# Layer 1's closing stage with tokens on partitions instead of model columns

## The reference

```python
out = moe_ffn(hl2, router_w[i], router_b[i], exp_w_gate[i], exp_w_up[i], exp_w_down[i],
              sh_w_gate[i], sh_w_up[i], sh_w_down[i])      # routed experts + shared expert
xl = xl + g2 * out.reshape(b, n_lat, d)                     # g2: one gate value per column
...
return rms_norm(xl, final_norm_w)

def routed_experts(...):      # per block of rows of one expert
    out = swiglu(h_pad[tok], e_gate[e], e_up[e], e_down[e])
    return y.at[tok].add(out * wt[:, None]), None

def rms_norm(x, w):
    y = xf * lax.rsqrt(jnp.mean(xf * xf, axis=-1, keepdims=True) + NORM_EPS)
    return y.astype(x.dtype) * w
```

## Time and profile before

| | us |
|---|---|
| Median of 3 runs (lowest, highest) | 2405.94 (2404.68, 2408.18) |
| The profiled execution | 2402.2 |
| Its span, first to last instruction | 2400.4 |
| PE busy | 2174.2 (91%) |
| DVE busy | 910.6 (38%) |
| ACT busy | 566.3 (24%) |
| POOL busy | 674.1 (28%) |

### The profile page before, as it was taken

How to read it: one execution, slowest core, us unless ns; L and a number is a source line. 1 busy time by engine, 2 the same in 40 slices (tenths; PEclk the granted TensorE clock), 3 DMA queues, 4 the chain that set the end, 5 groups by cost and what they waited for, 6 DMA issues and landing times.

```text
span 2400.4 us, 36613 instructions
## 1 busy us (share of the span) xinstructions
PE 2174.2 (91%) x12802; PEld 1173.2 (49%) x12802; DVE 910.6 (38%) x1858; ACT 566.3 (24%) x1170; POOL 674.1 (28%) x811
## 2 busy tenths in 40 slices
PE   4998989898899999999997798899879998888997
PEld 1464344454555555555546463354355454444545
DVE  2186676315512222222226485663352211111117
ACT  4222154304211111111113522342211111111113
POOL 0000000000245555555540000000045555555530
PEclk8999999998899999999999899999989999999999
DMA  7522000018699999999969121000159999999977
GB/s 317 221 78 75 0 1 1 1 35 333 240 376 418 420 412 408 408 409 418 412 266 326 53 91 37 1 1 18 70 236 397 417 416 414 409 408 409 413 295 245
DMA packets 104857, 594.23 MB, mean 248 GB/s; under 512 B 25142, under 2 KB 29374, under 8 KB 62528
## 3 DMA queue, kind: packets, MB, share of 16 engines
q1 hardware_dynamic: 68656, 524.73, 54.1%
q0 software_dynamic: 34672, 63.07, 7.0%
q10 hardware_dynamic: 1440, 5.24, 0.6%
HBM read 572.94 MB, written 60.56 MB: 264 GB/s over the span
## 4 chain that ended last, share of the span: by engine, by line
PE 68%; DMA 18%; DVE 7%; ACT 3%; issue 2%; SPq 1%; POOL 0%; POOLq 0%; DVEq 0%; ACTq 0%
PE psum L1056 22%; PE psum L704 18%; DMA arena<-in_experts 13%; PE psum L1078 10%; PE psum L875 3%; PE psum L899 2%; DMA arena<-y 2%; PE psum L915 2%; DMA arena<-in_mod_w 2%; PE psum L787 2%; PE psum L813 2%; PE psum L1064 1%; DVE arena L1544 1%; PE psum L720 1%; PE psum L1122 1%
## 5 line engine op out<-in xcount | busy, mean ns | idle before, releaser
L1056 PE MATMUL psum<-arena 128*64 128x256 f32 x6144 | 715.5, 386 | 39.2 <-DMA arena<-in_experts 31.2
L1056 PEld LDWEIGHTS psum<-arena 128*64 128x64 f32 x6144 | 440.4, 138 | 252.6 <-issue 43.6
L704 PE MATMUL psum<-arena 128*128 128x512 f32 (+1 forms) x1360 | 503.7, 528 | 24.9 <-ACT arena L1180 12.7
L2085 POOL DMA_INDIRECT arena<-hrows,IX x384 | 394.1, 1026 | 228.1 <-POOL IX L2081 163.1
L704 PEld LDWEIGHTS psum<-arena 128*128 128x128 f32 x1360 | 259.6, 193 | 264.1 <-issue 235.0
L1078 PE MATMUL psum<-arena 128*64 128x512 f32 x1536 | 363.5, 593 | 6.9 <-DMA arena<-in_experts 5.7
L2093 POOL DMA_INDIRECT y<-arena,IX x192 | 197.1, 1027 | 305.7 <-DVE arena L1929 146.2
L1936 DVE TENSOR_TENSOR arena<-psum,arena 128x128 f32<-128x128 f32 x192 | 55.9, 291 | 503.9 <-ACT arena L1420 503.9
L1420 ACT ACTIVATE arena<-psum 128x128 f32<-128x128 f32 x192 | 53.3, 278 | 667.6 <-PE psum L1056 667.6
L1428 ACT ACTIVATE arena<-psum 128x512 f32<-128x512 f32 x192 | 114.7, 597 | 310.7 <-PE psum L1078 310.7
L1078 PEld LDWEIGHTS psum<-arena 128*64 128x64 f32 x1536 | 112.8, 137 | 144.1 <-issue 119.8
(11 more groups left out here) (245 smaller groups left out, 1740.2 us busy)
## 6 DMA issues: line engine op xcount, KB each, us to landing
arena<-in_experts SPq DMA_DIRECT2D x128, 2048.0 KB, 20.9
arena<-in_experts SPq DMA_DIRECT2D x128, 1024.0 KB, 23.7
arena<-in_mod_w SPq DMA_DIRECT2D x48, 1024.0 KB, 11.1
arena<-y SPq DMA_DIRECT2D x20, 1536.0 KB, 15.6
arena<-in_wblk SPq DMA_DIRECT2D x22, 1024.0 KB, 4.9
arena<-in_shared SPq DMA_DIRECT2D x2, 3072.0 KB, 10.4
arena<-hrows,IX POOLq DMA_INDIRECT x384, 8.0
hrows<-arena ACTq DMA_DIRECT2D x10, 512.0 KB, 8.7
```

What stands on the lines that cost most here:

```text
L704: last = mm(job(l, key, n, parts), a, b, start=i == 0, stop=i == len(pairs) - 1)
L1056: last = mm(psum[j * ROWS:(j + 1) * ROWS, (0, 1, 5)[u], 0:2 * P], HT[:, u, k, :], w[:, k * 512 + j * 256:k * 512 + (j + 1) * 256], start=k ...
L2085: g.indirect_dma_start(GR[:, r, h * 256:(h + 1) * 256], None, rows, offsets(IX[:, s, h:h + 1]), bounds_check=4 * T * P - 1, oob_is_err=Fal ...
```

## The change

It concerns layer 1 alone, apart from the arrays handed over.

- A new job `gate` stands first in layer 1's shared list. PE spreads the gate's 1024 values over rows by 8 matmuls, with tokens' rows on partitions (64 rows for columns 0 to 511, 64 for 512 to 1023), and ACT copies them to `G2`. The banks of the jobs behind it are one further on.
- In layer 1's expert loop `weighted` is DVE's: it multiplies the down product by `G2` as it writes `YB`. ACT has only `gates` left. On DVE it stands between `hidden` and `hidden_in`.
- The final norm's weights come as 128 equal rows (`final`, 512 KB) and are loaded to `FW` ahead of y.
- A transfer of y carries three of the six rows of its block whole (runs of 1024 f32), not all six by half.
- PE transposes X for all four blocks into the eight PSUM banks (`xt`, bank 2t + i, 32 matmuls), and adds the sums to it there by 3 matmuls of 512 columns each half, tokens on partitions. `gated` is gone.
- The norm goes by token rows: ACT squares both banks at once and sums along the row, then a root of one column; DVE takes its reciprocal and makes two products of 512 columns from PSUM with `FW`. The block goes out in rows of 1024 f32.

```diff
@@ class Plan
+        self.shared += ["gate"] if l else []
         tiles(6)
...
-            j += [(("ct", t, i), "D") for i in range(2)]
-            if l == LAYERS - 1:
-                j += [(("nf", t), "A")]
+            j += [(("ct" if l == 0 else "xt", t, i), "D") for i in range(2)]
...
+            elif k[0] == "xt":
+                bk = 2 * k[1] + k[2]
@@ sync
+                if l == LAYERS - 1:
+                    sp.dma_start(FW, A["final"]).then_inc(sem("final_in"), 16)
+                for t in range(pl.t_out if l == LAYERS - 1 else 0):
+                    if t >= 3:
+                        ready(sp, l, ("xt", t - 3, 1))
+                    rows = y6d[l].rearrange("(k t p c) d -> t p k (c d)", k=TOPK, p=P, c=2)[t]
+                    for i in range(2):
+                        sp.dma_start(Y6[:, t % 3, 3 * i:3 * i + 3, :], rows[:, 3 * i:3 * i + 3, :]).then_inc(sem(f"y6in{t % 3}{i}"), 16)
...
-                sp.wait_ge(sem(f"norm_used{l}"), pl.norm[("nf", t)] + 1)
-                sp.dma_start(out[:, :, t * P:(t + 1) * P], H[:, :, t * P:(t + 1) * P]).then_inc(sem("out_done"), 16)
+                evacuated(sp, l, ("xt", t, 1))
+                sp.dma_start(out[t * P:(t + 1) * P, :], O[t]).then_inc(sem("out_done"), 16)
@@ tensor
+                    elif st == "gate":
+                        start_job(st)
+                        for m in range(KC):
+                            q = m // 4
+                            last = mm(psum[q * ROWS:(q + 1) * ROWS, pl.bank[st], (m % 4) * P:(m % 4 + 1) * P],
+                                      modTs[l][:, 5 * KC + m, 0:1].to_broadcast([P, ROWS]), ident, start=True, stop=True)
+                        last.then_inc(done, 1)
...
+                if l == LAYERS - 1:
+                    evacuated(pe, l, ("sd", KC - 1, 0))
+                    for t in range(pl.t_out):
+                        for i in range(2):
+                            start_job(("xt", t, i))
+                            for k in range(4):
+                                mm(job(l, ("xt", t, i))[:, k * P:(k + 1) * P], X[:, 4 * i + k, t * P:(t + 1) * P], ident,
+                                   start=k == 0, stop=False)
+                    for t in range(pl.t_out):
+                        for i in range(2):
+                            pe.wait_ge(sem(f"ysum{l}"), 2 * t + i + 1)
+                            for y in range(3):
+                                last = mm(job(l, ("xt", t, i)), ident, Y6[:, t % 3, y, i * 512:(i + 1) * 512], start=False, stop=y == 2)
+                            last.then_inc(done, 1)
@@ scalar
+                    elif st == "gate":
+                        ready(act, l, st)
+                        f(G2[:, :], job(l, st), ACT.Copy).then_inc(evacA, 1)
...
-                        for i in range(2):
-                            evacuated(act, l, ("ct", t, i))
-                            n = pl.square[("nf", t)][0] + i
-                            act.wait_ge(sem(f"sq_used{l}"), n - 2)
-                            f(SQB[:, n % 3, :].rearrange("p (k c) -> p k c", k=4), X[:, 4 * i:4 * i + 4, t * P:(t + 1) * P],
-                              ACT.Square).then_inc(sem(f"sq_ready{l}"), 1)
-                        root(("nf", t), P)
+                        ready(act, l, ("xt", t, 1))
+                        f(JUNK, psum[:, 2 * t:2 * t + 2, :].rearrange("p b n -> p (b n)"), ACT.Square, accum_out=ssq[:, t:t + 1]
+                          ).then_inc(sem("sum_made"), 1)
+                        act.wait_ge(sem("sum_made"), t + 1)
+                        f(rms[:, t:t + 1], ssq[:, t:t + 1], ACT.Sqrt, bias=epsb[:, 0:1], scale=1.0 / D).then_inc(sem("rms"), 1)
@@ vector
+                def weighted(s, i):
+                    dve.wait_ge(sem(f"down{l}"), i * n + (s + 1))
+                    r, u = tour.place(s, tour.y_ring)
+                    dve.wait_ge(sem(f"scat{r}_{l}"), i * 16 * tour.uses(r, tour.y_ring) + (16 * u + scat0))
+                    dve.sem_inc(sem("passed"), 1)
+                    V.tensor_tensor(YB[:, r, :], psum[:, (3, 4, 6)[tour.third(s)], :], G2[:, :], ALU.mult).then_inc(sem(f"y_a{l}"), 1)
...
                             hidden(ahead, i * n + (s + 1))
+                        if l:
+                            weighted(s, i)
+                        if not (last_round and ahead == 0):
                             hidden_in(ahead, i * n + (s + 1))
...
                 def last_norm(t):
-                    r = recip(("nf", t), P)
-                    for k in range(KC):
-                        last = V.scalar_tensor_tensor(H[:, k, t * P:(t + 1) * P], X[:, k, t * P:(t + 1) * P], pr(l, "final", k), r,
-                                                      ALU.mult, ALU.mult)
-                    last.then_inc(norm_used, 1)
+                    dve.wait_ge(sem("rms"), t + 1)
+                    link(V.reciprocal(rms[:, t:t + 1], rms[:, t:t + 1]))
+                    if t == 0:
+                        dve.wait_ge(sem("final_in"), 16)
+                    for i in range(2):
+                        V.scalar_tensor_tensor(O[t][:, i * 512:(i + 1) * 512], job(l, ("xt", t, i)), rms[:, t:t + 1],
+                                               FW[:, i * 512:(i + 1) * 512], ALU.mult, ALU.mult).then_inc(evacD, 1)
```

50 lines of the change are left out of this document (22 added, 28 removed).

## The result

| | before | after |
|---|---|---|
| median of 7 runs, us (lowest to highest) | 2405.94 (2401.39 to 2411.56) | 2394.81 (2390.99 to 2396.82) |
| the profiled execution, us | 2402.2 | 2394.81 |
| its span, us | 2400.4 | 2391.9 |

The ratio of the times is 0.995, with a 95% interval of 0.9937 to 0.9963: faster, by 11.1 us in the medians, where 5.8 had been forecast. The direction was right and the size was not: the time lies 0.7 us under the low end of the range. So the prediction was wrong in its number, and what has to be found is which terms of its sum were off.

What follows compares the result with a forecast made beforehand. The expert loop was taken as bound by its loads, the closing stage by the y loads and then DVE. Terms +1.8, +0.6, +1.3, -1.1, -8.4 sum to -5.8 us: 2405.9 to 2400.1, range 2395.5 to 2405.0.

Steps and rivals of the forecast that it cites:

- gate rows, at the loop's end: Layer 1's routing stage: the added gate matmuls on PE delay all routing, +1.8 us (0.9 to 1.9).
- eviction at the loop's end: Last pass of layer 1's expert loop: DVE's eviction delays the copy ahead of the last down product, +0.6 us (0.5 to 0.8).
- norm's weights ahead of y: Closing loads: 512 KB of norm weights on SP's queue delay the y transfers, +1.3 us (0 to 1.5).
- longer runs: Closing loads: y transfers in 4 KB instead of 2 KB runs go faster, -1.1 us (0 to -2.1).
- behind the last landing: From the last y landing to the end: 14.3 us in place of 22.7, so -8.4 us (-7.9 to -9.3).
- first rival: Closing loads: norm weights fall into the slow start and fewer descriptors cost less; -8.3 us in all, chance 0.18.
- all routing does later: Layer 1's routing: whatever PE does longer there delays all routing, priced at +1.8 us in the sum.
- the cover of the loop: Layer 1's expert loop: 3.1 us of cover lose 0.7 to DVE's eviction, which costs nothing until the loop's end.
- TensorE's clock: Closing stage rival: PE idles some 2.5 us between blocks, its clock drops for the last additions; -3.2 us in all, chance 0.17.
- The late loads: Closing stage rival: SP issues the last block's y loads late, after PE adds block 0; about -2.5 us in all, chance 0.10.

Runs made afterwards that it cites:

- d3: The kernel before with only layer 1's down-product eviction moved from ACT to DVE; 673.9 us from router to end, against 674.2 in the kernel before.
- c3: The changed kernel with the final norm's weights loaded during the expert loop instead of ahead of y; median 2397.98 us, ratio 0.9953 to the kernel before.
- c4: The changed kernel with y loaded by column halves in 2 KB runs, as before; median 2400.12 us, ratio 0.9957 to the kernel before.
- d1: The kernel before once more, word for word; 2400.49 us in its one run, 673.3 us from router to end.
- d2: The kernel before with only layer 1's y loads changed, to thirds in 4 KB runs; 674.1 us from router to end, against 674.2 in the kernel before.
- f1: The changed kernel with the early gate job's eight matmuls made four times over; 669.7 us from router to end, against 664.0 in the changed kernel.

## Why the prediction was wrong, step by step

Its sum of -5.8 stands against -10.2 from the router to the end of the span:

| term | forecast | shown |
|---|---|---|
| gate rows, at the loop's end | +1.8 | +1.6 in the routing, +2.7 at the loop's first product; +0.1 at the last down product, within the scatter |
| eviction at the loop's end | +0.6 | +0.6 in d3, +1.1 in after (0.5 of it the wait) |
| norm's weights ahead of y | +1.3 | +1.4 (c3 against after) |
| longer runs | -1.1 | -3.8 (c4 against after) |
| behind the last landing | -8.4 | -8.9 |

Up to SP's turn +1.2, the stream -3.8 + 1.4, the rest -8.9: -10.1 of the -10.2. Of the 4.4 us that the sum missed, 2.7 are in the longer runs, 1.2 in the two terms up to SP's turn and 0.5 behind the last landing.

**The step that failed is the price of the longer runs.** I took them as a matter of bandwidth once the stream runs: bytes by GB/s, with 388 before and 415 as the best. In the stream this was right (1.573 MB in 3.84 us is 410 GB/s, 0.21 to 0.24 a transfer against my best case of 0.26). But I left out that the first transfer, too, is made of those runs. It landed 8.7 behind SP's turn in before and 8.2 in d1, and 6.3 to 6.5 with 4 KB runs and nothing ahead of it (c3, d2). The prediction had even seen that "something there is not bandwidth", in its first rival, and then gave that 0.6 us and a chance of 0.18. This rival was right in that the start improves, and wrong on how: the weights don't fall into a slow start, they cost their full 1.4, and the start itself is shorter by 1.7 to 2.4. My range for this term ended at -2.1 and so could not reach -3.8.

The estimate by the Trainium skill's "DMA: Bandwidth & Descriptors", section "Why small descriptors are slow (HBM only)", was 0.7 for this term; a fixed cost a packet has the right sign, and the 5% between 4.05 and 3.84 is twice the 2.3% that it would make. The measured gap decides. With 0.7 in place of 1.1 the sum would have been -5.4, not the -5.3 that stands there.

**The gate rows** were priced rightly (1.6 for 1.8), and they do delay the routing. That "all routing does later" would reach the loop's end whole was only argued, and it is the second step that failed: +0.1 arrived. The prediction had said itself that the loop needs its loads, and had not asked what a later PE changes in them. PE then waits for the experts' weights from the 12th pass on, and before and after are within 0.1 us of each other at the end, while a shift that also moved the loads (f1, 3.0) arrived about whole.

**The eviction, and the cover of the loop:** d3 confirms both, with 0.5 in the wait and 0.63 up to SP's turn. In after it was 1.1 up to SP's turn; where the other 0.5 comes from isn't shown.

**Behind the last landing** the steps were sums 4.06 (measured 4.06), PE done at 7.4 (2385.70 - 2378.11 = 7.6), ACT to 9.0 (2387.16 - 2378.11 = 9.05), DVE to 10.7 (2388.81 - 2378.11 = 10.7), output 3.6 (2391.9 - 2388.81 = 3.1, before 3.9). So the whole chain held, and the output in 4 KB rows ended 0.5 sooner than I had taken.

**The rivals.** In after TensorE's clock stayed up (1.00 in 2378 to 2386), and PE idled 1.68 and 0.50 us ahead of the last two blocks, not 2.5: its additions of block 0 ended at 2367.56, not 2365.4, and left less idle behind them. The late loads didn't happen in after either, but did in c3, where 1.4 us less in the stream was enough. Both happened in f1, whose closing stage has the code of after: the last landing came 2.1 later, PE idled 2.14 us ahead of the last block, and its additions took 7.11 in place of 5.42, so that the stage took 52.1 and not 48.4. So neither rival is refuted. Each is a thing that the changed kernel misses by a narrow margin, and the -10.2 hold for the executions in which it does; four of the five profiles with this closing stage are such.

**The medians.** The forecast carried 3.7 us from the profiled execution to the median. The profiled execution of before was a short one (2402.2 where seven runs had 2405.94), and that of after was at its median. What differs between the profiled executions of one kernel lies for the most part ahead of the router (1726.2 and 1725.2, 1727.9 and 1725.7 against 674.2 and 673.3, 664.0 and 663.0), as far as two of each can tell. So to count from one profile was sound, and the -10.2 come out in the medians as -11.1, to within their interval.

## What to carry to other kernels

Price the start of a stream of transfers apart from its spacing, from issue to first landing, and let the row's run length bear on both: here over half of what longer runs gave (2.1 of 3.8) came before the first rows had landed. Shorten the engine work behind a stream first and its transfers second: the same edit of the loads was worth 0.6 us with the old tail and 3.3 with the new. And to see a gain of 5 to 10 us in a program whose runs differ by 10, cut the traces at marks in front of and behind the edited stage, and look at more than two executions: the closing stage repeated to 0.2 us in four of them and was 3.7 longer in the fifth. Before a term ahead of a loop is added to the end, ask what the loop waits for, PE or its loads.
